# Turning the second block's normed rows by a product with a diagonal of row factors

## What is computed

```python
def rms_norm_2(x, g):
    x32 = x.astype(jnp.float32)
    y = x32 * lax.rsqrt(jnp.mean(x32 * x32, axis=-1, keepdims=True) + NORM_EPS)
    return (y * g.astype(jnp.float32)).astype(x.dtype)

for l in range(DEPTH):                      # second_block, DEPTH = 2
    h = rms_norm_2(x, norm_mix[l])          # "mix"
    cols_a, cols_b, gate_a, gate_b = split_cols(h @ w_in[l], IN_SIZES)
    ...
    x = x + merged @ w_out[l]
    x = x + memory_attention(rms_norm_2(x, norm_mem[l]),           # "memx"
                             rms_norm_2(mem, mem_tok_norm[l]), ...)  # "memt"
    h = rms_norm_2(x, norm_ffn[l])          # "ffn"
    if l % 2 == 0:
        x = x + swiglu_2(h, ...)
    else:
        x = x + moe_swiglu(h, ...)          # eight experts, two for each token
```

## Time and profile before

| | us |
| --- | --- |
| median of three runs | 2706.18 |
| lowest, highest | 2704.82, 2706.55 |
| the profiled execution | 2707.27 |
| its span | 2705.4 |

### The profile page before, as it was taken

How to read it: one execution, slowest core, us unless ns; L and a number is a source line. 1 busy time by engine, 2 the same in 40 slices (tenths; PEclk the granted TensorE clock), 3 DMA queues, 4 the chain that set the end, 5 groups by cost and what they waited for, 6 DMA issues and landing times.

```text
span 2705.4 us, 38987 instructions
## 1 busy us (share of the span) xinstructions
PE 2609.6 (96%) x16908; PEld 2105.4 (78%) x16908; DVE 1558.5 (58%) x1690; ACT 1117.4 (41%) x1348; POOL 151.8 (6%) x121
## 2 busy tenths in 40 slices
PE   9999999999999999999989999999899899999998
PEld 8996687998989686997666769986576688787577
DVE  5455636456454745446874654458646457656477
ACT  5443534334434543434431444343314245454365
POOL 0002000000012100002011000010110000000000
PEclk9999999999999999999999999999999999999999
DMA  7653345657555254654531435554314167668886
GB/s 244 223 201 132 109 140 181 217 190 231 187 171 175 89 204 140 203 187 157 170 107 63 173 130 199 188 189 153 110 57 152 48 224 260 218 221 279 302 311 225
DMA packets 227742, 484.24 MB, mean 179 GB/s; under 512 B 11676, under 2 KB 45084, under 8 KB 227380
## 3 DMA queue, kind: packets, MB, share of 16 engines
q1 hardware_dynamic: 227572, 481.75, 52.4%
HBM read 477.01 MB, written 2.95 MB: 177 GB/s over the span
## 4 chain that ended last, share of the span: by engine, by line
PE 83%; DVE 10%; ACT 3%; issue 2%; DMA 1%; POOL 1%; SPq 0%; DVEq 0%; POOLq 0%; ACTq 0%
PE psum L780 19%; PE psum L448 12%; PE psum L450 12%; PE psum L449 12%; PE psum L451 10%; PE psum L498 4%; DVE weight_ring_low_halves L443 3%; PE psum L3438 2%; PE psum L2542 2%; PE psum L671 1%; PE psum L2628 1%; PE psum L515 1%; ACT weight_high_halves L437 1%; PE psum L3368 1%; POOL small L705 1%
## 5 line engine op out<-in xcount | busy, mean ns | idle before, releaser
L443 DVE TENSOR_TENSOR weight_ring_low_halves<-weight_ring,weight_high_halves 128x2048 fp32r<-128x2048 f32 (+1 forms) x330 | 735.9, 2238 | 484.0 <-ACT weight_high_halves L437 483.8
L437 ACT ACTIVATE weight_high_halves<-weight_ring 128x2048 fp32r<-128x2048 f32 (+2 forms) x343 | 637.4, 1867 | 508.9 <-PE psum L450 242.7
L448 PE MATMUL psum<-weight_high_halves,stage_area_halves 128*128 128x512 f32 (+4 forms) x1542 | 596.8, 387 | 18.4 <-DVE stage_area_halves L662 11.3
L450 PE MATMUL psum<-weight_high_halves,stage_area_halves 128*128 128x512 f32 (+4 forms) x1542 | 589.0, 382 | 0.0
L780 PE MATMUL psum<-stage_area_halves,weight_high_halves 128*128 128x256 f32 x2880 | 510.3, 281 | 0.0
L449 PE MATMUL psum<-weight_ring_low_halves,stage_area_halves 128*128 128x512 f32 (+4 forms) x1322 | 505.2, 382 | 0.0
L780 PEld LDWEIGHTS psum<-stage_area_halves,weight_high_halves 128*128 128x128 f32 x2880 | 441.8, 188 | 1.1
L780 PE MATMUL psum<-stage_area_halves,weight_ring_low_halves 128*128 128x256 f32 x1440 | 404.8, 281 | 0.0
L448 PEld LDWEIGHTS psum<-weight_high_halves,stage_area_halves 128*128 128x128 f32 x1542 | 290.4, 188 | 89.8 <-issue 17.6
L450 PEld LDWEIGHTS psum<-weight_high_halves,stage_area_halves 128*128 128x128 f32 x1542 | 290.4, 188 | 59.0
L451 PE MATMUL psum<-weight_ring,stage_area 128*128 128x512 f32 x704 | 307.8, 595 | 5.1 <-issue 4.1
(11 more groups left out here) (341 smaller groups left out, 2709.5 us busy)
## 6 DMA issues: line engine op xcount, KB each, us to landing
weight_ring<-in_ffn_w_up SPq DMA_DIRECT2D x44, 1024.0 KB, 5.1
weight_ring<-in_ffn_w_down SPq DMA_DIRECT2D x44, 1024.0 KB, 4.9
weight_ring<-in_ffn_w_gate SPq DMA_DIRECT2D x43, 1024.0 KB, 5.3
weight_ring<-in_w_in SPq DMA_DIRECT2D x38, 1024.0 KB, 6.7
weight_ring<-in_moe_wd SPq DMA_DIRECT2D x27, 1024.0 KB, 5.0
weight_ring<-in_moe_wu SPq DMA_DIRECT2D x25, 1024.0 KB, 6.8
weight_ring<-in_moe_wg SPq DMA_DIRECT2D x21, 1024.0 KB, 7.0
weight_ring<-in_mem_w_kv SPq DMA_DIRECT2D x16, 1024.0 KB, 5.1
```

What stands on the lines that cost most here:

```text
L437: act.raw.activation(high, whole, ACT.Copy).then_inc(*act.mark("high_halves", ("high", name)))
L443: v.raw.tensor_tensor(self.low_half(name), self.in_slot(name), self.high_half(name), ALU.subtract).then_inc(*v.mark("low_halves", ("halves ...
L448: pe.raw.matmul(out, a[1], w[0], start=start, stop=False)
L450: return pe.raw.matmul(out, a[0], w[0], start=False, stop=stop)
```

## The change

For `mix`, `memx` and `ffn` in both layers:
- VectorE multiplies x by the gain into `ax` (`scale_vector`, new), keeps the mean's step, and when GpSimd's factor is there makes a 128x128 diagonal of the row's factors out of the identity, into a new tile `row_scales`. In `memx` both rows are multiplied first, with their mean's steps, and both diagonals made then.
- PE turns a block with a plain fp32 product of the block (stationary) and the diagonal (moving) instead of the transpose with the identity. So the turned rows come out with their factor.
- The Square's elementwise result goes to a part of the stage area instead of `ax`, which now holds the gained rows at that time.
- `ax` holds rows without their factor. GpSimd multiplies it in (`rescale_gpsimd`, new) once the router has ranked the experts, and the first gather waits for that.

`memt` and the layer norms of the first block stay as they are.

```diff
@@ turn_tensor
             for i, block in enumerate(g["blocks"]):
-                mm = pe.raw.transpose(self.ps[:, g["bank"], i * P:(i + 1) * P], block, self.ident)
+                if "scales" in g:
+                    mm = pe.raw.matmul(self.ps[:, g["bank"], i * P:(i + 1) * P], block, g["scales"], start=True, stop=True)
+                else:
+                    mm = pe.raw.transpose(self.ps[:, g["bank"], i * P:(i + 1) * P], block, self.ident)
@@ class Second
+    def scale_vector(self, v, tag, j, rows=range(MT)):
+
+        net = self.net
+        v.wait_ge(*v.at(("loaded", tag)))
+        for m in rows:
+            v.raw.tensor_tensor(net.ax[:, m, :], net.x[:, m, :], net.norm_buf[:, j * D:(j + 1) * D], ALU.mult).then_inc(*v.mark("rows_gained", ("hn", tag, m)))
+            self.mean_vector(v, tag, m)
+        for m in rows:
+            v.wait_ge(*v.at(("rstd", (tag, m))))
+            v.raw.tensor_scalar(self.scales[m], net.ident, self.row_rstd[:, m:m + 1], None, ALU.mult).then_inc(*v.mark("row_scales_ready", ("scales", tag, m)))
...
+    def rescale_gpsimd(self, pool):
+
+        net = self.net
+        pool.wait_ge(*pool.at("ranked"))
+        for m in range(MT):
+            pool.wait_ge(*pool.at(*self.turn_need(("ffn", 1))[m]))
+            pool.raw.tensor_scalar(net.ax[:, m, :], net.ax[:, m, :], self.row_rstd[:, m:m + 1], None, ALU.mult).then_inc(*pool.mark("rows_rescaled", ("ax_normed", m)))
...
     def norm_turn(self, tag, src, dst):
         banks = (4, 5, 6, 7) if tag[0] in ("mix", "ffn") else (0, 1, 2, 3)
-        return self.net.turn_rows(("hT",) + tag, lambda m: src[:, m, :], KT, dst, lambda m: [("hn", tag, m)], banks=banks)
+        plain = tag[0] == "memt"
+        need = lambda m: [("hn", tag, m)] + ([] if plain else [("scales", tag, m)])
+        groups = self.net.turn_rows(("hT",) + tag, lambda m: src[:, m, :], KT, dst, need, banks=banks)
+        return groups if plain else [dict(g, scales=self.scales[g["name"][1]]) for g in groups]
@@ norm_rows_vector
         self.net.split_vector(v, pieces[:1])
-        self.rms_vector(v, tag, self.net.x, self.net.ax, j, [m])
+        self.scale_vector(v, tag, j, [m])
         self.net.split_vector(v, pieces[1:])
@@ Second.vector, memx
-            self.rms_vector(v, ("memx", l), net.x, net.ax, 1)
+            self.scale_vector(v, ("memx", l), 1)
@@ dispatch_tensor
-        pe.wait_ge(*pe.at(("slots", r)))
+        pe.wait_ge(*pe.at(("slots", r), ("ax_normed", 0), ("ax_normed", 1)))
```

More of the change, by code:

```diff
@@ L222, in __init__ @@
         self.small = sb("small", 1024)
+        self.row_scales = sb("row_scales", MT * P)
         self.x = self.x_buf[:, :].rearrange("p (m n) -> p m n", m=MT)
@@ L1936, in __init__ @@
             net.total, net.extra, net.inv = net.tiny(2, MT), net.tiny(2, MT), net.tiny(2, MT)
-        self.sq, self.row_rstd = net.tiny(MT), net.tiny(MT)
+        self.sq, self.row_rstd, self.unread = net.tiny(MT), net.tiny(MT), net.part(17408, MT, D)
+        self.scales = [net.row_scales[:, m * P:(m + 1) * P] for m in range(MT)]
         self.pos_i, self.pos = net.tiny(MT), net.tiny(MT)
@@ L2108, in load_rows, with rms_scalar, mean_vector @@
         self.net.load_param(name, self.net.norm_buf[:, j * D:(j + 1) * D], row_broadcast(src, D), after)
-    def rms_scalar(self, act, tag, src, dst, need, rows=range(MT)):
+    def rms_scalar(self, act, tag, src, need, rows=range(MT), unread=None):
+        unread = self.unread if unread is None else unread
         for m in rows:
             act.wait_ge(*act.at(*need(m)))
-            act.raw.activation(dst[:, m, :], src[:, m, :], ACT.Square, accum_out=self.sq[:, m:m + 1]).then_inc(*act.mark("rows_squared", ("squared", tag, m)))
+            act.raw.activation(unread[:, m, :], src[:, m, :], ACT.Square, accum_out=self.sq[:, m:m + 1]).then_inc(*act.mark("rows_squared", ("squared", tag, m)))
+    def mean_vector(self, v, tag, m):
+        v.wait_ge(*v.at(("squared", tag, m)))
+        v.raw.tensor_scalar(self.sq[:, m:m + 1], self.sq[:, m:m + 1], 1.0 / D, NORM_EPS, ALU.mult, ALU.add).then_inc(*v.mark("variance_ready", ("var", (tag, m))))
     def rms_vector(self, v, tag, src, dst, j, rows=range(MT)):
@@ L2119, in rms_vector @@
         for m in rows:
-            v.wait_ge(*v.at(("squared", tag, m)))
-            v.raw.tensor_scalar(self.sq[:, m:m + 1], self.sq[:, m:m + 1], 1.0 / D, NORM_EPS, ALU.mult, ALU.add).then_inc(*v.mark("variance_ready", ("var", (tag, m))))
+            self.mean_vector(v, tag, m)
             v.wait_ge(*v.at(("rstd", (tag, m)), ("loaded", tag)))
@@ L2895, in norm_rows_scalar @@
         for m in range(MT):
-            self.rms_scalar(act, tag, self.net.x, self.net.ax, lambda m: [("x", n, m)], [m])
+            self.rms_scalar(act, tag, self.net.x, lambda m: [("x", n, m)], [m])
             self.net.turn_copy(act, groups[m])
@@ L3018, in scalar @@
             net.split_scalar(act, later[1:2])
-            self.rms_scalar(act, ("memx", l), net.x, net.ax, lambda m: [("x", n + 1, m)])
+            self.rms_scalar(act, ("memx", l), net.x, lambda m: [("x", n + 1, m)])
             net.split_scalar(act, later[2:4])
@@ L3054, in vector @@
                 if (l, m) == (0, 1):
-                    self.rms_vector(v, ("mix", l), net.x, net.ax, 0, [m])
+                    self.scale_vector(v, ("mix", l), 0, [m])
                     net.split_vector(v, pieces[2:3])
```

4 lines of the change are left out of this document (3 added, 1 removed).

## The result

| | before | after |
| --- | --- | --- |
| median of 8 runs each, us | 2705.75 | 2713.34 |
| lowest, highest | 2703.61, 2709.27 | 2710.36, 2715.35 |
| profiled execution, its span | 2707.27, 2705.4 | 2714.89, 2713.1 |

The changed kernel is slower by 0.29%: ratio 1.0029, 95% interval 1.0020 to 1.0038. The forecast was 2707.3, 1.1 above the kernel before, with a range up to 2711.5; the changed kernel came out 7.6 above. Two later executions at a mean clock of 0.85, of some 2921 us, are left out of all that follows.

The account below looks back on a forecast made before the run. PE, busy 96% of the span, was taken as the bound, so time moves only where it waits or gets more work. Work +2.8 and clock -1.7 gave +1.1 on the median 2706.18: 2707.3 us, range 2703 to 2711.5.

Parts of the forecast that it names:

- The two records of a product, 1.95 for eight blocks: In every changed turn on PE, each product is two records; eight blocks take about 1.95 us, +0.86 a row.
- The chain to the first turn, 2.4 after x: In mix of layer 0, the first turn starts 2.4 us after x instead of 3.45, a chain shorter by 1.06.
- A product is four records: Rival for all turns on PE: a row pays 2.65 us instead of 0.86, giving 2729; chance 0.02.
- `mix` 0, -0.73: Two rows of mix, layer 0, where PE waits: 0.43 from VectorE free earlier and 0.30 net gain, -0.73 us.
- The clock behind `mix` 0, -1.7: Behind the second mix row of layer 0, the 3.4 us low-clock stretch goes and the clock stays up: -1.7 us.
- that the stretch goes elsewhere, 0.22: Rival: the low-clock stretch behind mix 0 stays or goes elsewhere, so only +2.8 us counts, 2709.0; chance 0.22.
- that longer waits bring more, 0.09: Rival: remaining waits and the longer key heads' wait bring two more low-clock stretches, +6.2 us, 2712.4; chance 0.09.
- The prediction's own sign of being wrong, low stretches other than two to four: In the profile after the change, a number of low-clock stretches other than two to four would show the prediction wrong.
- `memx`, +1.2 and +1.0: In memx of layers 0 and 1, longer turns delay ScalarE's copies and the key heads' norm: +1.2 and +1.0 us.
- `ffn` 0 and `mix` 1, first rows -0.2 and -0.1, second rows +0.86 each: First rows, where PE waits, gain 0.2 and 0.1 us; second rows, without a wait, pay 0.86 each.
- `ffn` 1, -0.05: In ffn of layer 1: first row -0.2 us, second row behind filler matmuls +0.15.
- GpSimd's rescaling, hidden: After the router ranks, two GpSimd passes of 2.35 us each, hidden behind expert 0; without cover up to 4.7.

Follow-up runs that it names:

- the 2 with the shorter pass: The changed kernel with one VectorE row-factor pass and transposes instead of diagonal products, without and with the key heads' norm moved ahead; 2703.45 and 2701.47 us.
- memx_only: The kernel before with only the four memx rows, both layers, turned by products; 2713.89 us, ratio 1.0028.
- the two fillers: memx_only and the whole changed kernel, each with 11 unread products added ahead of the key heads' turn in both layers; 2709.23 and 2710.89 us.
- heads_first: The changed kernel with memx's key heads' norm on VectorE moved ahead of the value weights' low halves; 2705.37 us, ratio 0.9991.
- memx_only_fill: memx_only with 11 unread products added ahead of the key heads' turn in both layers; 2709.23 us, ratio 1.0004.
- ffn1_only: The kernel before with only the ffn rows of layer 1 turned by products, with GpSimd's rescaling for the gather; 2707.90 us, ratio 1.0003.

## Why the prediction was wrong, point by point

All differences of place are of the two first profiles, after less before, with each step beginning where the last ended.

- **The two records of a product, 1.95 for eight blocks**: right. 192 records, 2.02 for eight.
- **The chain to the first turn, 2.4 after x**: right, 2.42. The diagonal took 0.29, not 0.22 (inside its bounds).
- **A product is four records**: this rival is out. Two records a block, and 2.02 against 1.09 for eight blocks is 1.9 times the transposes' time, not the four that the prediction quotes.
- **`mix` 0, -0.73**: wrong, -0.25 in the profile, +0.1 by the runs. Each row's halves come 0.89 and 0.90 later, not 0.76: the eight blocks take 2.02 and not 1.95, and ScalarE's copy alone takes 0.60, not half of the 1.08 that two in a row took. VectorE is free 0.26 earlier, not 0.43. A net of 0.3 between two terms near 1 had no room for errors of 0.1.
- **The clock behind `mix` 0, -1.7**: this is the single term that failed most. The stretch did go: it stands between 1237 and 1258 in 5 of the 7 profiles with before's norm and turn and no filler at this place, in 1 of the 2 with the shorter pass, and in none of the 7 with products. But the sum took it as won while everything else of the clock was kept as it was. Over 19 runs of the changed kernel and 121 of the kernel before the mean clock is 0.9961 and 0.9962, on one chip 0.9960 and 0.9965: at least as much came back as went. A part of it can come back behind the waits of 2.9 in `memx`: `memx_only` and the two fillers show that clock can be lost there; the two profiles of the changed kernel have one such stretch between them. The rest stays open. Both rivals on the clock (that the stretch goes elsewhere, 0.22, and that longer waits bring more, 0.09) had a part of the mechanism. The prediction's own sign of being wrong, low stretches other than two to four, came in the first profile of the changed kernel with five, and not in the second with four.
- **`memx`, +1.2 and +1.0**: right in place, chain and size. Ahead of the key heads' turn PE is 1.33 and 1.11 later. The wait grew by more (2.9, where 2.4 was forecast), since PE's own wait of 1.50 behind the turn of `memx` went. By `heads_first` this chain is what PE waits for. What the term left out is what such a wait can do to the clock; by the runs `memx` costs 3.4 to 4.4 at equal clock with it, and 1.4 where the wait is filled.
- **`ffn` 0 and `mix` 1, first rows -0.2 and -0.1, second rows +0.86 each**: right. -0.11 for the first, +0.81 for the next two together, then +0.9. The wait near 1835, 0.66 longer in this pair because two weight pieces kept ScalarE waiting 0.67 longer, had no term.
- **`ffn` 1, -0.05**: +0.2 by the second profile, +0.7 by the runs. Small, and its size isn't settled.
- **GpSimd's rescaling, hidden**: right. Two passes of 2.84 (not 2.35), done at 2174; the gather begins at 2260.
- **The sum**: the work is +4.9 along these profiles (-0.25, 1.33, -0.11, 0.81, 0.9, 0.66, 0.24 in a later wait, 1.11, 0.2) and +5.6 by the runs at equal clock, where +2.8 was forecast. The clock is between 0 and +0.9 (the means on one chip differ by 6.4), not -1.7. So the work's terms together miss at least as much as the clock's, with `mix` 0 and the wait near 1835 the largest (0.5 and 0.7). The profiles differ by 7.7, 2.8 more than the work; 1.2 of that stood already in front of the second block, in code that is the same in both, where the profile of after has the low stretch at 906 and that of before none.

The clock's price itself was counted as half a stretch's length. The Trainium skill (TensorE: Matmul & The Clock Gate, Terms) has the same, half of the throttled time at half the pulses. The runs give 0.64 of that. The rounding of the clock to 0.001 can account for under a tenth (the clocks of one kernel scatter by 0.001); that stretches lie partly over PE's idle time is a likely reason for the rest, and not shown.

## What to carry to other kernels

A low-clock stretch in one profile is a chance that has come true, not a cost that an edit can book whole: count it from the mean granted clock of many runs, and ask of every wait that an edit makes longer what the clock behind it will do. Where PE is busy 96% of the span, shortening a chain by giving PE work pays only if the halves behind it don't come later by nearly as much; first look for the cheaper operation on the engine that has room (here a pass with a row factor in 0.75 us), and then for a queue in which what PE waits for stands behind what it needs later.

## What the runs showed of the hardware that was not expected

- Products that nobody reads, put into a wait of 2.9 in each layer (`memx_only_fill`), brought the clock behind it from 0.50 to 1.00 and the mean of the runs from 0.9944 to 0.9963. The same wait in the changed kernel came with a low stretch behind it in one of four cases.
- A low stretch near 906, in code that all kernels share, is there in 6 of 17 profiles.
- A VectorE pass over 128x1024 with a row factor took 754 ns, a product of two tensors of this size 1.22 us, and the pass with a row factor over 128x128 286 ns.
- GpSimd's pass over 128x1024 with a row factor took 2.84 us.
- For the same two weight pieces of 1 MB ScalarE waited 1.90 us in one profile (`ffn1_only`) and 4.22 in another (`heads_first`), and in all 17 PE's wait some 20 us later was shorter than that by 1.5.
